# Retention encoder step: first gate tiles, VectorE combinations, split state terms and the places of o

## The reference

```python
h = rmsnorm(x, g)
p = h @ w_in                      # columns: hc, b, c, z_a, q, k, v, z_r, g_a, g_r
u = c * hc;  conv = 3 taps over u
a = ((b * conv) * silu(z_a)) @ w_a
q, k = rotary(q), rotary(k) * RET_DK ** -0.5          # 4 heads, 128 wide; v is 256 wide
scores = (q k^T) * decay          # per chunk
o = scores @ v + (q @ s_prev) * q_dec
s_new = gamma^L * s_prev + (k * k_dec)^T v
r = (head_norm(o) * silu(z_r)) @ w_r
x = x + (sigmoid(g_a) * a + sigmoid(g_r) * r) @ w_o
```

## Time and profile before

| | us |
|---|---|
| median of 3 runs | 2505.73 |
| lowest, highest | 2500.90, 2505.73 |
| the profiled execution's own time | 2498.74 |
| its span, first to last instruction | 2496.9 |
| PE busy in the span | 2320.6 (93%) |
| mean granted TensorE clock | 0.965 of full |

### The profile page before, as it was taken

One profiled execution on the slowest core, in us unless ns is written; L12 is line 12 of the kernel. 1 busy time (PEld: TensorE's weight loads), 2 busy tenths in 40 slices (PEclk: granted clock), 3 DMA queues, 4 the chain that ended last, 5 costly groups with the idle time before them and its releaser, 6 DMA issues.

```text
span 2496.9 us, 40347 instructions
## 1 busy us (share of the span) xinstructions
PE 2320.6 (93%) x16917; PEld 2288.0 (92%) x16917; DVE 1353.8 (54%) x1384; ACT 803.4 (32%) x1295; POOL 1164.6 (47%) x732
## 2 busy tenths in 40 slices
PE   6699999999999989599959999999999999976998
PEld 6699999999999888499959999999999998875998
DVE  5567777555543544344545767765666345434433
ACT  6333333444443312201233333334444442111000
POOL 3765656555554222144365655655555432221432
PEclk9799999999999999799979999999999999997999
DMA  8122222333332745744432222223333354554431
GB/s 274 45 69 61 69 61 70 111 118 122 123 121 65 269 149 178 103 148 122 127 120 69 61 70 61 70 78 123 123 123 123 105 192 159 204 90 131 142 131 72
DMA packets 260516, 290.35 MB, mean 116 GB/s; under 512 B 17168, under 2 KB 218096, under 8 KB 260336
## 3 DMA queue, kind: packets, MB, share of 16 engines
q1 hardware_dynamic: 260192, 287.73, 37.0%
q10 hardware_dynamic: 144, 0.05, 0.0%
HBM read 203.17 MB, written 84.57 MB: 115 GB/s over the span
## 4 chain that ended last, share of the span: by engine, by line
PE 86%; DVE 4%; POOL 3%; DMA 3%; ACT 2%; issue 2%; SPq 0%; DVEq 0%; POOLq 0%; ACTq 0%
PE ps L1401 58%; PE ps L1441 21%; DMA o_raw<-o_keep 2%; PE ps L1390 1%; DVE t_lo L1038 1%; DMA prod_raw<-prod_keep 1%; PE ps L1470 1%; PE ps L1529 1%; POOL power L674 1%; PE ps L1479 1%; DVE rstds L1167 1%; DVE o_lo L1200 0%; PE ps L1448 0%; PE ps L1450 0%; PE ps L1449 0%
## 5 line engine op out<-in xcount | busy, mean ns | idle before, releaser
L1401 PE MATMUL ps<-t_hi,s_hi 128*128 128x272 f32 x3920 | 814.2, 289 | 56.5 <-POOL s_lo L627 32.5
L1401 PE MATMUL ps<-t_hi,s_lo 128*128 128x272 f32 x3920 | 814.2, 289 | 0.0
L1401 PE MATMUL ps<-t_lo,s_hi 128*128 128x272 f32 x3920 | 811.0, 288 | 0.0
L1401 PEld LDWEIGHTS ps<-t_hi,s_hi 128*128 128x128 f32 x3920 | 619.6, 189 | 57.4 <-issue 32.8
L1401 PEld LDWEIGHTS ps<-t_lo,s_hi 128*128 128x128 f32 x3920 | 619.1, 189 | 0.0
L1401 PEld LDWEIGHTS ps<-t_hi,s_lo 128*128 128x128 f32 x3920 | 614.7, 190 | 0.0
L1069 DVE TENSOR_TENSOR e<-ps,snap 128x544 f32<-128x544 f32 x210 | 151.0, 722 | 502.4 <-PE ps L1401 352.5
L627 POOL TENSOR_TENSOR s_lo<-w_pair,s_hi 128x512 fp32r<-128x512 f32 x140 | 235.9, 1685 | 320.2 <-ACT s_hi L789 320.2
L799 ACT ACTIVATE snap<-ps 128x544 f32<-128x544 f32 x280 | 174.2, 622 | 449.4 <-PE ps L1401 449.0
L616 POOL TENSOR_TENSOR w_hi<-w_raw,zero 128x1024 fp32r<-128x1024 f32 x52 | 99.8, 1919 | 418.6 <-PE ps L1441 249.2
L638 POOL TENSOR_TENSOR sA<-w_pair 128x512 f32<-128x512 f32 x70 | 90.8, 1297 | 240.2 <-DVE s_lo L1056 240.2
(11 more groups left out here) (221 smaller groups left out, 3619.3 us busy)
## 6 DMA issues: line engine op xcount, KB each, us to landing
w_pair<-in_w_in_dram SPq DMA_DIRECT2D x140, 512.0 KB, 5.0
xs<-x_keep SPq DMA_DIRECT2D x16, 544.0 KB, 4.9
prod_keep<-e SPq DMA_DIRECT2D x16, 544.0 KB, 2.7
v_keep<-e SPq DMA_DIRECT2D x16, 544.0 KB, 6.0
z_keep<-e SPq DMA_DIRECT2D x16, 544.0 KB, 4.1
prod_raw<-prod_keep SPq DMA_DIRECT2D x16, 544.0 KB, 9.3
vT<-v_keep SPq DMA_DIRECT2D x16, 544.0 KB, 7.6
U<-ga_keep SPq DMA_DIRECT2D x16, 544.0 KB, 4.7
```

The source lines that it names most:

```text
L1401: i = mm(ps[:, r + p, 0:PART], s[j][:, k, :], b[operand][:, k, p * PART:(p + 1) * PART], start=(FRESH[j] and k == 0 and t == 0), stop=(k = ...
```

## The change

NG, the number of plain gate tiles at the start of a layer, goes from 2 to 4, so that g_a and g_r of block 1 leave the pairs (34 pairs, an even number). The combinations of h move from POOL to DVE; ACT scales only the upper half of x, and DVE puts the gain of the lower half into them, so that the last has the other sign. In the heads, DVE takes the low part of k before `normalise` and `gate_a`. q has one buffer instead of two and is loaded after the last outputs of the head before; q and S are split, and q by S becomes three products. prod lies in the places of T1 to T4, and waits for later products of the last pair. State, k and v move to the first places, o is made in place of z, and SP loads o tiles 0 to 2 within the last head and 4, 5 and 3 right behind it, ahead of the convolution rows, which now come after the first two merge loads. PE takes r's tiles in another order.

```diff
+NG = 4
-    + [("G", m) for m in range(1, KT)]
+    + [("G", m) for m in range(NG // 2, KT)]
-U_G, U_A, U_R, U_O, NU = 0, 2, 10, 18, 26
+U_G, U_A, U_R, U_O, NU = 0, NG, NG + 8, NG + 16, NG + 24
...
-        prod = split_tiles("prod", [a + j * 2 * TILE for a in (QB11, QB21, QT, QT + QUAD) for j in range(2)])
+        prod = split_tiles("prod", [QT + k * 2 * TILE for k in range(KT)])
...
@@ SP
                 load_xs(l, 1)
                 load_pair(l, 1)
+                for idx in range(2, NG):
+                    load_unit(l, U_G + idx)
                 load_xs(l, 2)
+                store_gate(l, 0)
+                load_xs(l, 3)
+                store_gate(l, 1)
                 load_pair(l, 0)
-                load_xs(l, 3)
...
-                    sp.wait_ge(product_done, 7 * last_pair + (M1, M2, M5, M6)[k // 2] + 1)
+                    sp.wait_ge(product_done, 7 * last_pair + (M5, M6, M7, M4)[k // 2] + 1)
...
+                    sp.wait_ge(c_done, hn * NC_ + C_X + 1)
                     if h < HEADS - 1:
-                        sp.wait_ge(c_done, hn * NC_ + C_X + 1)
                         load_kv(l, h + 1)
-                        load_q(l, h + 1)
+                    else:
+                        load_o(l, 0)
+                        load_o(l, 1)
+                        sp.wait_ge(c_done, hn * NC_ + C_S + 1)
+                        sp.wait_ge(q_split, hn + 1)
+                        load_o(l, 2)
                     sp.wait_ge(sample_state, hn + 1)
...
                         load_state(l, h + 1)
+                        sp.wait_ge(b_done, hn * NB + S_O + 1)
+                        load_q(l, h + 1)
+                sp.wait_ge(b_done, (l * HEADS + HEADS - 1) * NB + S_O + 1)
+                load_o(l, 4)
+                load_o(l, 5)
+                sp.wait_ge(states_stored, 32 * HEADS * (l + 1))
+                load_o(l, 3)
+                store_a(l, KT - 1)
+                load_merge(l, 0)
+                load_merge(l, 1)
                 sp.wait_ge(conv_kept, KT * (l + 1))
...
-                sp.wait_ge(o_stored, 32 * (HEADS - 1) * (l + 1))
-                sp.wait_ge(unit_done, l * NU + U_A + KT)
-                for k in range(6):
...
-                store_a(l, KT - 1)
-                load_merge(l, 0)
-                load_merge(l, 1)
@@ POOL
-                combine(l, 0)
-                combine(l, 1)
-                combine(l, 2)
-                prepare_first(l, 0)
-                combine(l, 3)
-                prepare_second(l, 0)
-                for n in range(1, NP):
+                for idx in range(2, NG):
+                    split(l, U_G + idx)
+                for n in range(NP):
@@ ACT
+                    high_q(l, h)
                     act.wait_ge(decayed_ready, hn + 1)
...
+                    high_state(hn, 0)
+                    high_state(hn, 1)
@@ DVE
+            def combine_t(l, k):
+                a, b = xs[1 - k % 2]
+                gain = par[:, PG + l * KT + k + 4:PG + l * KT + k + 5]
+                dve.wait_ge(xs_scaled, 4 * l + k + 1)
...
+                tt(t1, b12, b11, ALU.subtract).then_inc(t_added, 1)
+                stt(t3, x22, gain, b12, ALU.mult, ALU.subtract).then_inc(t_added, 1)
+                stt(t2, x22, gain, t1, ALU.mult, ALU.subtract).then_inc(t_added, 1)
+                stt(t4, x21, gain, t2, ALU.mult, ALU.subtract).then_inc(t_added, 1)
...
+                for k in range(4):
+                    combine_t(l, k)
+                    low_t(l, k)
+                    if k < 2:
+                        gate_first(l, k)
+                for i in range(2, NG):
+                    gate_first(l, i)
...
                         mean(hn - 1, 2, P, 4, 4)
-                        gate_a(l, 2 * h - 1)
-                        normalise(hn - 1, 2, P, 4, 4, by_value(sm_b))
...
                     stt(K_lo[:, :, :], by_chunk(sm_a), hc[:, h, KDEC:KDEC + 1], K_hi[:, :, :].bitcast(F32),
                         ALU.mult, ALU.subtract).then_inc(a_free, 1)
+                    if h:
+                        normalise(hn - 1, 2, P, 4, 4, by_value(sm_b))
+                        gate_a(l, 2 * h - 1)
...
                     gate_a(l, 2 * h)
+                    dve.wait_ge(q_high, hn + 1)
+                    tt(q_lo[:, :], qT[:, 0:SEQ], q_hi[:, :].bitcast(F32), ALU.subtract).then_inc(q_split, 1)
...
+                        if c == 4:
+                            low_state(hn, 0)
+                        scan(l, h, c).then_inc(scanned, 1)
                         dve.wait_ge(scanned, hn * NCH + c + 1)
+                    low_state(hn, 1)
@@ PE
+                if i_ >= 2:
+                    pe.wait_ge(g_scaled, 16 * l + i_ - 1)
...
                 if n == 0:
-                    pe.wait_ge(g_scaled, 16 * l + 1)
+                    pe.wait_ge(g_scaled, 16 * l + NG - 1)
...
-                        i = mm(out[:, c % 4, :], qT[h % 2][:, c * CHUNK:(c + 1) * CHUNK], S[:, c - 1, :], start=False, stop=True)
+                        mm(out[:, c % 4, :], q_hi[:, q], S_hi[:, c - 1, :], start=False, stop=False)
+                        mm(out[:, c % 4, :], q_hi[:, q], S_lo[:, c - 1, :], start=False, stop=False)
+                        i = mm(out[:, c % 4, :], q_lo[:, q], S_hi[:, c - 1, :], start=False, stop=True)
...
-                r_tiles(0, range(4))
-                turn_output_sample(hn)
-                turn_output(hn, 0)
-                turn_output(hn, 1)
-                r_tiles(0, (4, 5))
+                r_tiles(0, range(3))
                 pe.wait_ge(weights_split, u + 2)
...
-                r_tiles(1, range(6))
+                r_tiles(1, (0,))
+                turn_output_sample(hn)
+                turn_output(hn, 0)
+                r_tiles(1, (1,))
+                turn_output(hn, 1)
+                r_tiles(1, (2,))
+                r_tiles(0, (3, 4, 5))
+                r_tiles(1, (3, 4, 5))
```

More of the change, by code:

```diff
@@ L99 @@
 DVE_OUTS = [sum(len(stores_of(i)) for i in range(n) if PAIRS[i][0] != "G") for n in range(NP + 1)]
-ACT_OUTS = [2 + sum(len(stores_of(i)) for i in range(n) if PAIRS[i][0] == "G") for n in range(NP + 1)]
+ACT_OUTS = [NG + sum(len(stores_of(i)) for i in range(n) if PAIRS[i][0] == "G") for n in range(NP + 1)]
 def pair_count(l, n):
@@ L188, in build @@
         gate_in = [place(f"a_in{j}", [P, COLS], F32, offset=snaps_at + j * TILE) for j in range(2)]
-        o_out = [place(f"o_out{v}", [P, COLS], F32, offset=snaps_at + v * TILE) for v in range(2)]
+        S_hi = place("S_hi", [P, NCH - 1, DV], F32R, offset=snaps_at)
         sums_at = at[0]
@@ L194, in build @@
         hc = place("hc", [P, HEADS, NHC], F32, offset=sums_at)
+        junk = [place(f"junk{c}", [P, DV], BF16, offset=sums_at + HEADS * NHC * 4 + c * 512) for c in range(4)]
+        at[0] = max(at[0], sums_at + HEADS * NHC * 4 + 2048)
         rs_at = at[0]
@@ L214, in build @@
         vT = [place(f"vT{v}", [P, COLS], F32, offset=QB22 + (1 + v) * TILE) for v in range(2)]
[L215 to L218, removed]
+        qT = place("qT", [P, COLS], F32, offset=QB22 + 3 * TILE)
+        q_hi = place("q_hi", [P, SEQ], F32R, offset=raw_at + 2 * P * KT * 4)
+        q_lo = place("q_lo", [P, SEQ], F32R, offset=raw_at + 2 * P * KT * 4 + SEQ * 4)
         z = [place(f"z{v}", [P, COLS], F32, offset=QB12 + v * TILE) for v in range(2)]
@@ L224, in build @@
         Pr_lo = place("Pr_lo", [P, NCH, CHUNK], F32R, offset=ring + 6 * 4096)
[L225 to L236, removed]
+        v0_at = QB11
+        k_at = v0_at + (NCH + 1) * DV * 4
+        s_at = k_at + (NCH + 1) * DK * 4
+        v1_at = s_at + (NCH + 2) * DV * 4
+        assert v1_at + (NCH + 1) * DV * 4 <= QB22
+        V_hi = [place(f"V_hi{b}", [P, NCH, DV], F32R, offset=a) for b, a in enumerate((v0_at, v1_at))]
+        V = [place(f"V{b}", [P, NCH + 1, DV], F32, offset=a) for b, a in enumerate((v0_at, v1_at))]
+        K_hi = place("K_hi", [P, NCH, DK], F32R, offset=k_at)
+        K = place("K", [P, NCH + 1, DK], F32, offset=k_at)
+        S = place("S", [P, NCH + 2, DV], F32, offset=s_at)
+        S_lo = place("S_lo", [P, NCH - 1, DV], F32R, offset=s_at)
+        o = split_tiles("o", [QB22, QB11, QB22 + 2 * TILE, QB11 + 2 * TILE, QB12 + 2 * TILE, ring + 4 * 4096,
+                              QB21, QB21 + 2 * TILE])
         a_out = X1
@@ L409, in load_q @@
                 kept_there(sp, "q", l, h)
[L410 removed]
+                sp.dma_start(qT[:, :], kept["q"][h]).then_inc(q_loaded, 16)
             def load_z(l, h):
@@ L758, in scale_xs @@
                 act.wait_ge(xs_loaded[b], 32 * (2 * l + k // 2 + 1))
-                for j in range(2):
-                    m = PG + l * KT + k + 4 * j
-                    do(xs[b][j][:, :], xs[b][j][:, :], ACT.Copy, scale=par[:, m:m + 1]).then_inc(xs_scaled, 1)
+                m = PG + l * KT + k
+                do(xs[b][0][:, :], xs[b][0][:, :], ACT.Copy, scale=par[:, m:m + 1]).then_inc(xs_scaled, 1)
             def high_t(l, k):
@@ L947, in _ @@
```

(10 more changed lines are left out.)

188 lines of the change are left out of this document (95 added, 93 removed).

## The result

The changed kernel takes 2377.99 us (median of 4 runs, 2367.36 to 2389.12) against 2503.35 for the kernel before: a ratio of 0.950, 95% interval 0.9454 to 0.9546. The forecast was 2379, with 2359 to 2408 as its range. The profiled execution is the fastest of the four, 2367.36 us with a span of 2365.6.

What follows compares the result with a forecast made beforehand. PE, with 86% of the chain, and the gaps in its work bound the kernel. Gains of 48.6 + 25.9 + 2 + 0 + 48 = 124.5 from 2498.74 give 2374, plus 4.6 makes 2379 us, range 2359 to 2408.

Steps and rivals of the forecast that it cites:

- Layer start: Start of each layer: PE's waits and slow starts mostly go, less added work and a remaining wait; 48.6 us gained.
- the remaining wait: Layer start: PE still waits 2.5 us for DVE's scaling, plus a slow start of 1.5: 4.0 per layer.
- rival 1: Layer start: DVE stands still while POOL runs, 6.7 us of wait each, 2387 or 2392 us; chance 0.16.
- Heads: Heads: 25.9 us from six waits for k's low part, 2 from q by S, 0 from pairs to heads.
- Rival 2: Heads: the wait moves to `normalise`, 2 us in six heads, 2391 us; chance 0.08.
- rival 5: Heads: with one buffer q lands too late and PE waits, slower at 2510 us; chance 0.03.
- Rival 4: Layer start: the gap is x arriving, not POOL's order, so half of 56.6 us stays, 2407; chance 0.03.
- r stage: First load of o to third r unit: o no longer waits behind the convolution stores; 48 us gained over both layers.
- PE's own path: r stage: PE's copies, row tiles, turns and split waits up to the third unit take 41 us.
- The load: r stage: third unit's weights, behind the convolution stores, decide; with the split 43.0 and 46.0 us in the layers.
- the 4 us for merge loads and four issues: r stage: SP's time for three merge loads and four store issues, part of 15 us before the weights' load.
- the 4.6 us carried over from the kernel before: Final sum: 4.6 us added to 2374 because the runs shown lie 2.2 to 7.0 above the profiled execution.

Runs made afterwards that it cites:

- The order experiment: Changed kernel with the low part of k put back behind `normalise` and `gate_a`: median 2400.82 us, 22.8 us more.
- the first execution: The unedited changed kernel's first profiled execution, fastest of its four: 2367.36 us, span 2365.6.
- the second: The changed kernel run again with no edit, its profiled execution: span 2380.1 us, median 2376.93.

## Why the prediction was right, and where not

**Layer start, 48.6 forecast, 52.7 measured.** The term too large was the remaining wait: 4.0 per layer. PE's first product of the pairs, in layers 0 and 1:

```profile
81.77 0.52 PE L1448 MATMUL ps<-t_hi,s_hi 128*128 128x272 f32 x2 [2.48 <-DVE U L1083]
```

```profile
1240.90 0.53 PE L1448 MATMUL ps<-t_hi,s_hi 128*128 128x272 f32 x2 [0.44 <-DVE U L1083]
```

Layer 0 is as worked out, 2.5 and a slow start of 1.6; in layer 1 POOL's first split ends early in VectorE's chain, and 0.4 and 0.2 are left. That is 3.3 of the 4.1 us by which the gain was short. The price of POOL beside VectorE can now be read, on DVE's timeline of layer 0 (first the operations beside a split, then the same ones alone) and POOL's.

```profile
45.33 2.42 DVE L1061 SCALAR_TENSOR_TENSOR t_raw<-xs,par,t_raw 128x544 f32<-128x544 f32 x1
47.77 2.80 DVE L1063 SCALAR_TENSOR_TENSOR t_raw<-xs,par,t_raw 128x544 f32<-128x544 f32 x1
...
68.55 0.78 DVE L1061 SCALAR_TENSOR_TENSOR t_raw<-xs,par,t_raw 128x544 f32<-128x544 f32 x1
69.36 0.79 DVE L1063 SCALAR_TENSOR_TENSOR t_raw<-xs,par,t_raw 128x544 f32<-128x544 f32 x1
```

```profile
45.21 1.95 POOL L642 TENSOR_TENSOR w_hi<-w_raw,zero 128x1024 fp32r<-128x1024 f32 x1 [15.71 <-DMA w_raw<-in_w_in_dram]
47.24 2.75 POOL L644 TENSOR_TENSOR w_lo<-w_raw,w_hi 128x1024 fp32r<-128x1024 f32 x1
```

POOL's operation starts first each time, and VectorE's ends 0.59 and 0.58 us after it (47.75 against 47.16, 50.57 against 49.99): VectorE stands still, which is rival 1's mechanism. That agrees with the Trainium skill, *SBUF — State Buffer*, section "SBUF: two separate sides", by which the one that starts first keeps the shared port for its whole instruction. But over layer 0 it costs six rows 1.64 + 2.01 + 1.64 + 2.02 + 1.04 + 1.08 = 9.4 us, near the forecast's 8.3 and not the 13 that rival 1 counts, so that the wait is 2.5 us and not 6.7.

**Heads, 25.9 + 2 and 0 forecast, 28.3 measured.** The order experiment gives 24.4 for the low part of k, 25.9 forecast. Over the same stretch the kernel before takes another 3.2 + 0.2 = 3.4 us: q by S in three products with all the rest, 2 forecast, and no run shows the products alone. From the end of the pairs to the first turn of head 1 it takes 46.09 before and 46.02 after, in layer 1 46.20 and 45.71: 0, as forecast. Rival 2 did not come: `turn_output` waits 0.5 us, as before. Nor did rival 5: PE never waits for q. Rival 4 is out by the layer starts.

**r stage, 48 forecast, 50.4 in the profiled execution.** Here the step was right in kind and mis-sized in its parts. The forecast counts from the end of the last a unit, 970.88 in layer 0 and 2129.32 in layer 1; the last output, where the table cuts, is 2.9 us later. From there to the third unit PE's own path, 41 forecast, takes 1014.63 − 970.88 = 43.8 and in layer 1 43.2, but 1011.72 − 970.65 = 41.1 in layer 0 of the run with the stores moved. What the sum left out is the low clock after the wait for the second unit's split, which lasted longer in the first two (last section).

The load was to be issued after 15 us and to land 22.66 or 25.71 later. In layer 0 it was issued after 19.0 in one execution and 29.2 in the other, and landed 18.8 and 19.0 later. In the first execution two misses cancel, so that its 43.8 stands beside the forecast's 43.0; in the second the third unit starts 1023.70 − 971.04 = 52.7 us after the last a unit. The term that failed is the 4 us for merge loads and four issues: they took 989.90 − 982.45 = 7.5 and 1000.23 − 982.90 = 17.3. The four issues had taken 2.3 us in the kernel before, and I did not see that a store's issue itself can hold SP, here one of them for 12.20.

These late loads fit the 10.6 us between the profiled execution and the median. The number to doubt was not a gain but the 4.6 us carried over from the kernel before, whose runs shown ahead lie within 7 us (2498.74 to 2505.73), while nine on another chip spread over 14.5 (2493.22 to 2507.69).

## What to carry to other kernels

When two releases of a stage lie within a few us of each other, a single profile shows one of them, and removing either alone gains nothing in it: compare the spread of the runs, and take both away. Many-element stores are to be counted by what they do to their queue, to the issuing engine and to all that follows; here one at a time among the pairs was the best place. A gap at a start is closed by cover work and by a shorter chain together; price each with the other undone.

## What the runs showed of the hardware beyond that

The four convolution stores are 4 KB each, in 4-byte elements. In the kernel before, and in the run with o loaded behind them, each issue held SP 0.45 to 0.66 us. Behind the merge loads, where seven of the kernels have them, the third held SP 3.16 us at the least and 12.20 at the most, in the same program at the same place. That the transfers ahead of them make the difference is likely, but no run changes that alone.

Four of them draining beside the pairs went with a standstill of PE, VectorE and ACT of some 7 us in layer 1 of one run and 2.9 us at the same place of another, and with none in layer 0; one at a time the pairs of layer 1 took at most 0.9 us more than in the changed kernel. The Trainium skill, *Runtime: NRT & Kernel Launch*, section "Instruction fetch mechanics", says that each engine fetches its code in blocks by a DMA queue of its own. The DMA view of the 25 us around the 7 us (1786 to 1811), and of the same stretch with the stores one by one, lists the queues with packets, MB and their share of the engines' time:

```profile
q1 hardware_dynamic: 6435, 1.86, 129.3%
```

```profile
q1 hardware_dynamic: 4471, 3.32, 43.4%
q8 instruction: 1, 0.02, 0.3%
```

In the first no packet of q8 starts between 1785.51 and 1811.55, while elsewhere in these pairs they come some 16 us apart: code did come late there, by some 10 us. But PE ran steadily again from 1809.92, ahead of that packet, and ACT and VectorE had stood since 1799.8 and 1800.6, before PE stopped at 1803.4. Late code alone does not explain that, and the cause stays open.

After the same wait of 4.08 and 4.07 us for the second unit's split, the granted clock stayed low for different times. First PE's rows behind that wait, in the changed kernel and in the run with the stores moved.

```profile
984.03 1.27 PE L1488 MATMUL ps<-o_hi,w_hi 128*128 128x364 f32 x3 [4.08 <-POOL w_lo L644]
```

```profile
983.79 1.28 PE L1488 MATMUL ps<-o_hi,w_hi 128*128 128x364 f32 x3 [4.07 <-POOL w_lo L644]
```

Then the windows of the changed kernel and of the run with the stores moved (columns: window, us, then busy time of PE, PEld, DVE, ACT and POOL with instructions, the granted clock, DMA share, GB/s):

```profile
985.00:997.00 12.00, 10.47 (x47) 9.50 (x45) 4.13 (x6) 1.24 (x2) 0.00 (x0) 0.64 1.11 104
```

```profile
985.00:997.00 12.00, 10.46 (x63) 9.50 (x62) 7.04 (x8) 2.11 (x2) 0.00 (x0) 0.92 0.41 147
```

A mean of 0.64 against 0.92 of full speed, between the levels of 1.2 and 2.4 GHz: the lower one, with 3.1 us for a row tile in place of 1.5, held through two tiles and two turns in one execution and through one tile in the other, worth 2.7 us to the third unit (from the last output 1014.63 − 973.76 = 40.9 against 1011.72 − 973.53 = 38.2 us). What decides it is open.
